# Emptying each tile of the feed-forward's up projection one tile later on VectorE

## Chip, core and metric

The kernel runs on one core of a Trainium2 chip. The metric is the device time of one execution in microseconds (us). Before the change, three runs gave a median of 3300.18 us (3292.87 to 3311.64).

## What is computed

The reference is a stack of transformer-like blocks on 512 tokens of width 1024. Two layers each end in a gated feed-forward of width 2752 with a short causal convolution (three taps over tokens), and this is the part that the change touches:

```
def conv_glu_ffn(xn, w_up, conv_w, conv_b, w_down):
    u, gt = split_cols(xn @ w_up, (D_FF, D_FF))
    u = causal_dwconv(u, conv_w, conv_b)
    return (jax.nn.silu(u) * gt) @ w_down
```

Before it, xn is a root-mean-square norm of the residual. The two layers have the same shapes. What follows them (a retention and attention block with a mixture of experts) is not touched.

## The kernel before

All is kept with features on the 128 partitions and 512 tokens along the free axis. A float32 product is made of three passes of the rounded format fp32r: the high part of the weights by the high part of x, high by low, and low by high. One **tile** of a projection is 128 output features by 512 tokens: 8 blocks of 128 input features by 3 passes, so 24 matmuls into one PSUM bank (`tile_products`, line 335 for the matmul). A weight chunk for one tile is 128x1024 values, 512 KB, loaded by SyncE into a ring of four (line 3361).

Each chunk is split on two engines before TensorE can use it. ScalarE casts it to its high part (`chunk_high`, line 302), and VectorE subtracts that from the chunk to get the low part, the **remainder** (`chunk_rest`, line 308). The split halves live in `chunk_split`, which has two places: the cast of chunk j therefore waits until tile j-2 has been multiplied. TensorE starts tile j when chunk j's remainder is done and one of four PSUM banks, used in turn, is free.

The up projection of a layer has 44 tiles, in groups of four: two tiles of u (the convolved half), then the two matching tiles of the gate. VectorE empties tile j in `up_out(j)` (lines 1467 to 1479). It first multiplies the bank by the norm's reciprocal roots into a scratch tile (line 1470). For a u tile it then makes the three taps of the convolution (lines 1473 to 1475), about 2.8 us in all; for a gate tile it multiplies by silu of the matching u tile into `hidden` (line 1478), about 1.4 us. The last instruction frees the bank (`bank_free`). ScalarE takes silu of a u tile in `silu_of(j)` (line 1407), once `up_out(j)` has freed its bank.

The order of the work is written out by hand, by engine. On VectorE (loop at lines 1502 to 1511), iteration j does the remainder of chunk j, then `up_out(j - 1)`, then at one iteration in four from j = 14 the low part of a finished hidden tile for the down projection (`x_rest`, line 322), and in 24 of the iterations one `ada_reduce` (lines 1018 to 1026: two instructions over a loaded 512 KB unit of another matrix). On ScalarE (loop at lines 1413 to 1426), iteration j casts chunk j, then takes silu of tile j-2, then at one iteration in four from j = 13 the high part of a hidden tile (line 314). At j = 2 ScalarE takes the square roots of the norm and VectorE turns them into reciprocals (line 396), so tiles 0 and 1 can be emptied only after that. Five times within the 44 tiles TensorE runs eight very narrow matmuls on the reduced unit (`ada_tile`, line 1035), and after tile 0 the norm's sum (line 379). GpSimd loads the units for `ada_reduce` (line 1006), each when an earlier unit has been used.

The down projection follows without a break (line 1376 is its matmul). Its first three output banks are others than the four of the up projection; before its fourth, TensorE waits for the last `up_out` (line 1366).

Of the kernel before, what the change touches and what calls it, by code (L numbers as in the profile page):

```python
# [155 lines left out]
def program(nc, d, out):  # L156

    ctx = ExitStack()
    with ctx:
# [55 lines left out]
        def vec(name, j=0, n=1):  # L215
            return vecs[:, VEC_AT[name] + j:VEC_AT[name] + j + n]
# [37 lines left out]
        def flat(ap):  # L254
            return ap.rearrange("p a b -> p (a b)")
# [41 lines left out]
        def chunk_high(act, lin, j):  # L297
            n = lin.c0 + j
            act.wait_ge(landed[n % RING], 16 * (n // RING + 1))
            act.wait_ge(chunk_used.sem, n + 1)  # L300
            at = (n % 2) * KB * P
            act.copy(chunk_split[:, 0, at:at + KB * P], flat(ring[:, n % RING])).then_inc(chunk_hi.sem, 1)  # L302

        def chunk_rest(dve, lin, j):
            n = lin.c0 + j
            dve.wait_ge(chunk_hi.sem, n + 1)
            at = (n % 2) * KB * P
            dve.tensor_tensor(chunk_split[:, 1, at:at + KB * P], flat(ring[:, n % RING]), chunk_split[:, 0, at:at + KB * P],  # L308
                              ALU.subtract).then_inc(chunk_taken.sem, 1)

        def x_high(act, lin, k, x, gain=None):
            dst = lin.split[0][k][:, 0:lin.tokens]
            if gain is None:
                act.copy(dst, x).then_inc(x_hi.sem, 1)
            else:
                act.activation(dst, x, ACT.Identity, scale=gain).then_inc(x_hi.sem, 1)
# [43 lines left out]
        def square(act, norm, k, x):  # L360
            act.activation(norm.squares[k][:, 0:norm.tokens], x, ACT.Square).then_inc(sq_ready.sem, 1)
# [24 lines left out]
        def take_roots(act, norm):  # L386
            act.wait_ge(sum_ready.sem, norm.b_sum + 1)
            ins = act.activation(norm.roots, banks[:, norm.bank, 0:norm.tokens], ACT.Sqrt, bias=eps[EPS], scale=1.0 / D)
            if norm.by_token is not None:
                ins = act.activation(norm.by_token, banks[:, norm.bank + 1, 0:norm.tokens // P], ACT.Sqrt, bias=eps[EPS],  # L390
                                     scale=1.0 / D)
            ins.then_inc(root_ready.sem, 1)
# [911 lines left out]
        def layer_end(layer, after=None):  # L1304
# [4 lines left out]
            n_up, n_down = 2 * FF_TILES, KB * DOWN_CHUNKS  # L1309
# [85 lines left out]
            def act(act):  # L1395
                if layer == 0:
                    act.activation(cond, vec("c", 0, 8), ACT.Silu).then_inc(cond_ready, 1)

                def prepare(j):
                    act.wait_ge(bank_free.sem, out.freed(j))  # L1400
                    x_high(act, up, j, x[j], gain[j])
                    square(act, norm, j, x[j])

                def silu_of(j):
                    if j % 4 < 2:
                        act.wait_ge(bank_free.sem, up.freed(j))
                        act.activation(silu[:, j % 4, :], conv[:, j % 4, :], ACT.Silu).then_inc(silu_ready.sem, 1)

                attention_act(act)
                for j in range(2, KB):  # L1410
                    chunk_high(act, out, j)
                    prepare(j - 2)
                for j in range(n_up):
                    chunk_high(act, up, j)
                    if j < 2:
                        prepare(KB - 2 + j)
                    elif j == 2:
                        take_roots(act, norm)
                    else:
                        if j == 3:  # L1420
                            silu_of(0)
                        silu_of(j - 2)
                    if j % 4 == 1 and 3 <= j // 4 < 11:
                        k = j // 4 - 3
                        act.wait_ge(bank_free.sem, up.freed(hidden_tile(k)))
                        x_high(act, down, k, hidden[:, k, :])
                for c in range(n_down):
                    g, m = c // KB, c % KB
                    chunk_high(act, down, c)
                    if g + 1 < DOWN_CHUNKS and m:  # L1430
                        for k in ks(g + 1):
                            if min(k % KB, KB - 2) == m - 1:
                                act.wait_ge(chunk_used.sem, down.used(KB * g - 1))
                                act.wait_ge(bank_free.sem, up.freed(hidden_tile(k)))
                                x_high(act, down, k, hidden[:, k, :])
                    if after and g == DOWN_CHUNKS - 1 and m >= 2:
                        next_x(act, m - 2)
                    if first and g == DOWN_CHUNKS - 1 and m >= 2:
                        first.square(act, m - 2)
                if first:  # L1440
                    first.act(act)
                if after:
                    beside = mixer.act(act, next_lin.freed)
                    for j in range(next_lin.n):
                        chunk_high(act, next_lin, j)
                        if j < 2:
                            next_x(act, KB - 2 + j)
                        elif j == 2:
                            take_roots(act, next_norm)
                        if j == 3 or j >= act_from:  # L1450
                            next(beside, None)
                    for _ in beside:
                        pass
# [6 lines left out]
            def dve(dve):  # L1460
# [6 lines left out]
                def up_out(j):  # L1467
                    i, n, bank, y = j // 4, j % 4, up.bank(j), turned[j % 2]
                    dve.wait_ge(chunk_used.sem, up.used(j))
                    L(dve.tensor_tensor(y, bank, norm.roots, ALU.mult))  # L1470
                    if n < 2:
                        c, w = conv[:, n, :], [vec(f"ffn_cw{layer}", 2 * i + n + FF_TILES * back) for back in range(3)]
                        L(dve.tensor_scalar(c, y, w[2], vec(f"ffn_cb{layer}", 2 * i + n), ALU.mult, ALU.add))
                        L(dve.scalar_tensor_tensor(c[:, 1:T], y[:, 0:T - 1], w[1], c[:, 1:T], ALU.mult, ALU.add))  # L1474
                        ins = dve.scalar_tensor_tensor(c[:, 2:T], y[:, 0:T - 2], w[0], c[:, 2:T], ALU.mult, ALU.add)
                    else:
                        dve.wait_ge(silu_ready.sem, base + 2 * i + n - 1)
                        ins = dve.tensor_tensor(hidden[:, 2 * i + n - 2, :], silu[:, n - 2, :], y, ALU.mult)
                    ins.then_inc(bank_free.sem, 1)
# [22 lines left out]
                for j in range(2, n_up):  # L1502
                    chunk_rest(dve, up, j)
                    if j == 2:
                        invert_roots(dve, norm)
                        up_out(0)
                    up_out(j - 1)
                    if j % 4 == 2 and 3 <= j // 4 < 11:
                        x_rest(dve, down, j // 4 - 3, hidden[:, j // 4 - 3, :])
                    for u in range(units_by(j - 1), units_by(j)):  # L1510
                        ada_reduce(dve, first_unit + u)
                dve.sem_inc(down_started, 1)
                chunk_rest(dve, down, 0)
                up_out(n_up - 1)
                for c in range(1, n_down):
                    g, m = c // KB, c % KB
                    chunk_rest(dve, down, c)
                    if g + 1 < DOWN_CHUNKS and m:
                        for k in ks(g + 1):
                            if min(k % KB, KB - 2) == m - 1:  # L1520
                                x_rest(dve, down, k, hidden[:, k, :])
                    if c == 3:
                        modulation(dve, layer)
                        if first:
                            first.constants(dve)
                    if g == DOWN_CHUNKS - 1 and m:
                        add_down(m - 1)
                        if after and m >= 2:
                            x_rest(dve, next_lin, m - 2, x[m - 2], next_gain[m - 2])
                            add_square(dve, next_norm, m - 2)  # L1530
                        if first and m >= 2:
                            first.add(dve, m - 2)
# [2017 lines left out]
```

## Time and profile before

| | |
|---|---|
| median of three runs | 3300.18 us (3292.87 to 3311.64) |
| span of the profiled execution, first to last instruction | 3300.1 us |
| first up projection (first matmul of it to first matmul of the down projection) | 618.48 to 873.18 us |
| second up projection | 1404.28 to 1658.88 us |
| TensorE busy over the span | 3120.8 us (95%) |
| VectorE busy over the span | 2292.4 us (69%) |

The profile gives the profiled execution's own time only as its span, 3300.1 us; that is 0.1 us under the median run, so sums against the one hold for the other. Engines are PE (TensorE), PEld (its weight load), DVE (VectorE), ACT (ScalarE), POOL (GpSimd) and SP (SyncE). In a timeline, a bracket at the end of a row gives how long the engine sat idle before it and which instruction released it; rows that follow each other on one line are merged with their count.

### The profile page before, as it was taken

Reading aid. Unit: us, or ns where it says so; the run is one execution under the profiler, and the core shown is the slowest. Engines: PE = TensorE matmul, PEld = TensorE weight load, DVE = VectorE, ACT = ScalarE, POOL = GpSimd, SP = SyncE. Lnnn points to the kernel's source line nnn. Section 1 sums busy time; section 2 is a strip of 40 time slices with the busy share of each in tenths; the row PEclk is TensorE's granted clock in tenths of the full one; section 3 lists DMA queues with packets and bytes.
Section 4 is the critical chain, followed back from the end, with each engine's and each line's share of the span. In section 5 each row is a group of like instructions: output and inputs, shape, how many; then the busy total and the mean of one; then the engine's idle time right before and its main releaser. Section 6 shows DMA issues by size and latency. Waiting matters only on the chain.

```text
span 3300.1 us, 44885 instructions
## 1 busy us (share of the span) xinstructions
PE 3120.8 (95%) x17105; PEld 2537.3 (77%) x17105; DVE 2292.4 (69%) x2269; ACT 1566.1 (47%) x1574; POOL 183.8 (6%) x214
## 2 busy tenths in 40 slices
PE   8979699999999789999999988889999999999998
PEld 7859587787887578778887766677888888888886
DVE  4664455677545654577735456679999999999997
ACT  3343233322234342422223224467777777777775
POOL 0000000000000000000000000101111111111110
PEclk9989899999999889999999997899999999999999
DMA  4210032344322112334323210679999999999996
GB/s 158 84 44 4 27 115 90 118 149 141 125 102 90 39 64 96 121 122 148 133 96 121 89 39 28 242 281 398 383 393 382 384 392 383 384 392 383 384 392 227
DMA packets 119374, 638.92 MB, mean 194 GB/s; under 512 B 13480, under 2 KB 13480, under 8 KB 69456
## 3 DMA queue, kind: packets, MB, share of 16 engines
q1 hardware_dynamic: 99168, 561.05, 44.1%
q0 software_dynamic: 20080, 76.04, 7.6%
q8 instruction: 97, 1.59, 0.2%
q14 instruction: 29, 0.24, 0.0%
HBM read 612.92 MB, written 24.12 MB: 193 GB/s over the span
## 4 chain that ended last, share of the span: by engine, by line
PE 86%; DVE 10%; ACT 1%; DMA 1%; issue 1%; PEldq 0%; DVEq 0%; SPq 0%; PEld 0%; POOL 0%; ACTq 0%; POOLq 0%
PE banks L335 31%; PE banks L2985 21%; PE banks L3002 10%; PE banks L1376 7%; PE banks L348 3%; PE banks L1834 3%; DVE chunk_split L308 1%; PE banks L2970 1%; PE banks L776 1%; PE banks L799 1%; PE banks L2991 1%; PE banks L2234 1%; DVE scratch L1474 1%; DVE scratch L396 1%; DVE scratch L1470 0%
## 5 line engine op out<-in xcount | busy, mean ns | idle before, releaser
L335 PE MATMUL banks<-x_scratch,chunk_split 128*128 128x512 f32 x3648 | 851.3, 394 | 36.3 <-DVE x_scratch L322 22.7
L335 PEld LDWEIGHTS banks<-x_scratch,chunk_split 128*128 128x128 f32 x3648 | 687.3, 189 | 193.1 <-issue 48.6
L302 ACT CAST chunk_split<-weight_ring 128x1024 fp32r<-128x1024 f32 x292 | 306.3, 1049 | 952.2 <-PE banks L335 719.2
L2985 PE MATMUL banks<-pair_split,rows 128*128 128x512 f32 x3072 | 717.2, 394 | 5.2 <-DVE pair_split L2633 3.5
L2985 PEld LDWEIGHTS banks<-pair_split,rows 128*128 128x128 f32 x3072 | 578.7, 189 | 137.9 <-issue 7.5
L308 DVE TENSOR_TENSOR chunk_split<-weight_ring,chunk_split 128x1024 fp32r<-128x1024 f32 x292 | 357.1, 1223 | 216.2 <-ACT chunk_split L302 207.1
L3002 PE MATMUL banks<-pair_split,hidden_t 128*128 128x512 f32 x1536 | 360.3, 393 | 2.5 <-DVE pair_split L2633 2.1
L3002 PEld LDWEIGHTS banks<-pair_split,hidden_t 128*128 128x128 f32 x1536 | 284.3, 188 | 65.5 <-DVE pair_split L2633 3.8
L2633 DVE TENSOR_TENSOR pair_split<-weight_ring,pair_split 128x2048 fp32r<-128x2048 f32 x128 | 290.4, 2289 | 35.9 <-ACT pair_split L2628 35.9
L2633 DVE TENSOR_TENSOR pair_split<-scratch,pair_split 128x2048 fp32r<-128x2048 f32 x128 | 290.5, 2289 | 31.1 <-ACT pair_split L2628 30.8
L2633 DVE TENSOR_TENSOR pair_split<-mixed,pair_split 128x2048 fp32r<-128x2048 f32 x128 | 291.3, 2290 | 24.6 <-ACT pair_split L2628 24.6
L2628 ACT CAST pair_split<-scratch 128x2048 fp32r<-128x2048 f32 x128 | 244.2, 1907 | 59.1 <-PE banks L2985 57.5
L2628 ACT CAST pair_split<-weight_ring 128x2048 fp32r<-128x2048 f32 x128 | 241.4, 1911 | 61.5 <-PE banks L2985 51.5
L2628 ACT CAST pair_split<-mixed 128x2048 fp32r<-128x2048 f32 x128 | 245.1, 1916 | 49.1 <-PE banks L2985 48.6
L1470 DVE TENSOR_TENSOR scratch<-banks,scratch 128x512 f32<-128x512 f32 x88 | 60.7, 690 | 119.1 <-PE banks L335 119.0
L1376 PE MATMUL banks<-x_down_hi,chunk_split 128*128 128x512 f32 x448 | 141.5, 395 | 0.0
L3240 POOL DMA_INDIRECT token_sums<-normed,tables x31 | 84.3, 2720 | 335.1 <-ACT normed L3078 302.8
L1376 PEld LDWEIGHTS banks<-x_down_hi,chunk_split 128*128 128x128 f32 x448 | 84.2, 188 | 19.7
L335 PE MATMUL banks<-x_mix,chunk_split 128*128 128x512 f32 x384 | 92.1, 399 | 0.0
L335 PE MATMUL banks<-x_queries,chunk_split 128*128 128x512 f32 x384 | 91.7, 397 | 0.0
L335 PE MATMUL banks<-x_proj,chunk_split 128*128 128x512 f32 x384 | 90.4, 397 | 0.0
L1376 PE MATMUL banks<-x_down_lo,chunk_split 128*128 128x512 f32 x224 | 88.2, 394 | 0.0
(661 smaller groups left out, 3581.0 us busy)
## 6 DMA issues: line engine op xcount, KB each, us to landing
weight_ring<-in_weights SPq DMA_DIRECT2D x292, 512.0 KB, 3.2
mixed<-in_w SPq DMA_DIRECT2D x128, 1024.0 KB, 7.5
weight_ring<-in_w SPq DMA_DIRECT2D x128, 1024.0 KB, 8.1
scratch<-in_w SPq DMA_DIRECT2D x128, 1024.0 KB, 8.9
mixed<-in_w_ada POOLq DMA_DIRECT2D x48, 512.0 KB, 3.8
token_sums<-tables POOLq DMA_DIRECT2D x1, 2560.0 KB, 9.3
residual<-in_x POOLq DMA_DIRECT2D x4, 512.0 KB, 6.6
projected<-in_mem POOLq DMA_DIRECT2D x2, 1024.0 KB, 5.2
```

The costliest lines, as they stand in the source:

```text
L302: act.copy(chunk_split[:, 0, at:at + KB * P], flat(ring[:, n % RING])).then_inc(chunk_hi.sem, 1)
L308: dve.tensor_tensor(chunk_split[:, 1, at:at + KB * P], flat(ring[:, n % RING]), chunk_split[:, 0, at:at + KB * P], ALU.subtract).then_inc( ...
L335: mm = pe.matmul(lin.bank(j), chunk_split[:, a, at + k * P:at + (k + 1) * P], lin.split[b][k][:, 0:lin.tokens], start=(k, a, b) == (0, 0, ...
L348: mm = pe.matmul(banks[:, into[tt], :], lin.split[b][k][:, tt * P:(tt + 1) * P], chunk_split[:, a, at:at + T], start=(k, a, b) == (0, 0, 0 ...
L1376: mm = pe.matmul(banks[:, DOWN_BANKS[m], :], chunk_split[:, a, at + (k % KB) * P:at + (k % KB + 1) * P], down.split[b][k], start=(k, a, b) ...
L1470: L(dve.tensor_tensor(y, bank, norm.roots, ALU.mult))
L1834: ins = pe.matmul(out(tt, c), lhs(tt, c), rhs(tt, c), start=True, stop=True)
L2628: act.copy(pair_split[s][:, 0, :], raw[r]).then_inc(pair_hi, 1)
L2633: dve.tensor_tensor(pair_split[s][:, 1, :], raw[r], pair_split[s][:, 0, :], ALU.subtract).then_inc(pair_lo, 1)
L2985: mm = pe.matmul(banks[:, n, :], rows[:, a, k, :], pair_split[k % SLOTS][:, b, n * T:(n + 1) * T], start=False, stop=(k, a) == (KB - 1, 1))
L3002: mm = pe.matmul(banks[:, 4 + n, :], hid_t[:, a, k, :], pair_split[c][:, b, at:at + T], start=(k, a, b) == (0, 0, 0), stop=(k, a) == (KB - ...
L3240: pool.indirect_dma_start(sums, bass.IndirectOffsetOnAxis(row_out, 0), y_tok, None, compute_op=ALU.add)\
```

## The change

On VectorE, iteration j empties tile j-2 in place of tile j-1. The reciprocal at j = 2 is followed by `up_out(0)` alone. The last two tiles go behind the remainders of the down projection's chunks 0 and 1. On ScalarE, silu follows one tile later too, and that of tile 41 goes behind the down projection's first cast. No instruction is added or removed.

```diff
@@ ScalarE @@
                     elif j == 2:
                         take_roots(act, norm)
                     else:
-                        if j == 3:
-                            silu_of(0)
-                        silu_of(j - 2)
+                        silu_of(j - 3)
...
                     chunk_high(act, down, c)
+                    if c == 0:
+                        silu_of(n_up - 3)
@@ VectorE @@
                     chunk_rest(dve, up, j)
                     if j == 2:
                         invert_roots(dve, norm)
-                        up_out(0)
-                    up_out(j - 1)
+                    up_out(j - 2)
...
                 dve.sem_inc(down_started, 1)
                 chunk_rest(dve, down, 0)
-                up_out(n_up - 1)
+                up_out(n_up - 2)
                 for c in range(1, n_down):
                     g, m = c // KB, c % KB
                     chunk_rest(dve, down, c)
+                    if c == 1:
+                        up_out(n_up - 1)
```

## Rows read from the trace of the kernel before

**Rows 1.** The page: busy time by engine, and the chain that ended last, by engine.
```profile
PE 3120.8 (95%) x17105; PEld 2537.3 (77%) x17105; DVE 2292.4 (69%) x2269; ACT 1566.1 (47%) x1574; POOL 183.8 (6%) x214
...
PE 86%; DVE 10%; ACT 1%; DMA 1%; issue 1%; PEldq 0%; DVEq 0%; SPq 0%; PEld 0%; POOL 0%; ACTq 0%; POOLq 0%
```

**Rows 2.** Windows, the two up projections: us, busy by engine, PEclk, DMA share, GB/s.
```profile
618.48:873.18 254.70, 247.87 (x1100) 202.22 (x1098) 185.14 (x237) 68.59 (x79) 11.61 (x22) 1.00 0.40 132
1404.28:1658.88 254.60, 247.77 (x1100) 202.23 (x1099) 185.14 (x237) 68.60 (x79) 10.57 (x20) 1.00 0.39 132
```

**Rows 3.** Waits in the first up projection: us in total, times, longest us.
```profile
POOL mixed L1006 <- DVEq L1028: 246.9, 20, 73.0
ACT chunk_split L302 <- PE banks L335: 150.7, 44, 5.7
DVE scratch L1470 <- PE banks L335: 59.3, 30, 3.8
...
PE banks L335 <- DVE chunk_split L308: 6.7, 9, 1.6
```

**Rows 4.** Groups of TensorE instructions in the second up projection: busy, mean ns | idle before.
```profile
L335 PE MATMUL banks<-x_scratch,chunk_split 128*128 128x512 f32 x1056 | 244.3, 391 | 6.8 <-DVE chunk_split L308 6.7
```

**Rows 5.** Timeline in the first up projection, start of the part with the reciprocal.
```profile
624.22 1.05 ACT L302 CAST chunk_split<-weight_ring 128x1024 fp32r<-128x1024 f32 x1 [3.29 <-PE banks L335]
...
625.37 1.23 DVE L308 TENSOR_TENSOR chunk_split<-weight_ring,chunk_split 128x1024 fp32r<-128x1024 f32 x1 [1.48 <-ACT chunk_split L302]
...
627.30 3.35 DVE L396 RECIPROCAL scratch<-scratch 128x512 f32<-128x512 f32 x1 [0.70 <-ACT scratch L388]
...
630.65 1.05 ACT L302 CAST chunk_split<-weight_ring 128x1024 fp32r<-128x1024 f32 x1 [3.38 <-PE banks L335]
...
636.21 1.22 DVE L308 TENSOR_TENSOR chunk_split<-weight_ring,chunk_split 128x1024 fp32r<-128x1024 f32 x1
...
637.58 12.73 PE L335 MATMUL banks<-x_scratch,chunk_split 128*128 128x512 f32 x55 [1.58 <-DVE chunk_split L308]
...
643.37 1.05 ACT L302 CAST chunk_split<-weight_ring 128x1024 fp32r<-128x1024 f32 x1 [5.48 <-PE banks L335]
```

**Rows 6.** Timeline, same stage, around a tile with the most VectorE work.
```profile
745.56 0.69 DVE L1470 TENSOR_TENSOR scratch<-banks,scratch 128x512 f32<-128x512 f32 x1 [1.46 <-PE banks L335]
745.62 1.05 ACT L302 CAST chunk_split<-weight_ring 128x1024 fp32r<-128x1024 f32 x1 [1.98 <-PE banks L335]
...
748.33 0.68 DVE L322 TENSOR_TENSOR x_down_lo<-projected,x_down_hi 128x512 fp32r<-128x512 f32 x1
748.45 0.63 ACT L1407 ACTIVATE scratch<-scratch 128x512 f32<-128x512 f32 x1 [1.78 <-DVE scratch L1475]
748.93 0.74 DVE L1020 SCALAR_TENSOR_TENSOR scratch<-mixed,tables,scratch 128x512 f32<-128x512 f32 x1
749.71 0.75 DVE L1022 SCALAR_TENSOR_TENSOR scratch<-mixed,tables,scratch 128x512 f32<-128x512 f32 x1
750.61 1.23 DVE L308 TENSOR_TENSOR chunk_split<-weight_ring,chunk_split 128x1024 fp32r<-128x1024 f32 x1
...
751.06 1.05 ACT L302 CAST chunk_split<-weight_ring 128x1024 fp32r<-128x1024 f32 x1 [1.98 <-PE banks L335]
...
751.98 8.22 PE L335 MATMUL banks<-x_scratch,chunk_split 128*128 128x512 f32 x35 [1.02 <-DVE chunk_split L308]
752.47 0.69 DVE L1478 TENSOR_TENSOR projected<-scratch 128x512 f32<-128x512 f32 x1
...
757.80 1.05 ACT L302 CAST chunk_split<-weight_ring 128x1024 fp32r<-128x1024 f32 x1 [5.69 <-PE banks L335]
```

**Rows 7.** Timeline of ScalarE, same stage: two casts with a narrow-matmul tile between them.
```profile
728.34 1.05 ACT L302 CAST chunk_split<-weight_ring 128x1024 fp32r<-128x1024 f32 x1 [2.52 <-PE banks L335]
734.74 1.05 ACT L302 CAST chunk_split<-weight_ring 128x1024 fp32r<-128x1024 f32 x1 [5.34 <-PE banks L335]
```

**Rows 8.** Waits of the SyncE queue in the first up projection: us, times, longest us.
```profile
SPq L3361 <- DVE chunk_split L308: 227.6, 44, 10.3
```

## The prediction

> **What bounds the kernel now.** I read the page first: TensorE is busy for 95% of the span, and 86% of the chain that ended last is TensorE's [rows 1]. So the change can be worth no more than TensorE's pauses in the stretches that it touches, unless it makes new ones. Those stretches are the two up projections. I took their windows from the first matmul of the up projection to the first of the down projection: 254.70 and 254.60 us, at a granted clock of 1.00, with VectorE busy for 185.14 us of each, 73% [rows 2]. Neither engine is full.
>
> The waits of the first stretch say what stops TensorE there: nine waits, 6.7 us in all, all on VectorE's remainder (line 308). The other way round, line 1470, the first instruction that empties a tile, waited 59.3 us for TensorE in 30 of its 44 times [rows 3]. So VectorE first waits for a tile to end, then empties it, and only then does the remainder that TensorE will need next. The second stretch has the same 6.7 us [rows 4].
>
> The timeline of a heavy tile shows the order [rows 6]. The tile ends at about 745.56. ScalarE casts the next chunk from 745.62 to 746.67, so its remainder could follow then. VectorE instead empties the tile until 748.33, makes the low part of a hidden tile until 748.93 and two instructions for the other matrix until 750.6, and does the remainder from 750.61 to 751.84. TensorE finished its tile in the meantime (the cast at 751.06 shows it) and starts the next at 751.98 only.
>
> **What these waits cost.** The casts mark the ends of tiles, since each waits for one. Undisturbed they are 5.44 us apart (745.62 to 751.06); after the late remainder the distance is 6.74 us (751.06 to 757.80), so a recorded idle time of 1.02 us cost 1.30 [rows 6]. The difference is overlap between matmuls of neighbouring tiles that is lost too. I therefore take the loss from the stretch, not from the idle times:
> - 44 tiles x 5.44 = 239.36 us
> - five tiles with the narrow matmuls behind them: 6.40 us between casts (728.34 to 734.74 [rows 7]), 0.96 more than 5.44, so 4.80 us
> - the norm's sum behind tile 0: 630.65 - 624.22 = 6.43 [rows 5], so 0.99 us
> - left of 254.70: 9.55 us; of 254.60: 9.45 us.
>
> Together **19.0 us** are due to late remainders, against 13.4 us of recorded idle (2 x 6.7). Of each 9.5, 1.84 us lie at the start, where two tiles took 643.37 - 630.65 = 12.72 us: there the reciprocal (3.35 us) and the emptying of tiles 0 and 1 all stand ahead of the remainder of chunk 3, which starts at 636.21 [rows 5].
>
> **The change, part by part.** No instruction is added or removed; the order changes.
>
> *VectorE, the steady loop.* After the remainder of chunk j, VectorE now empties tile j-2, which ended before that remainder could start. It no longer waits for tile j-1, and the next remainder has only that work ahead of it. Count from a cast's start at the end of tile j-2. The remainder is ready 2.38 us later (cast at 624.22, remainder to 626.60 [rows 5]). The heaviest work behind it is 5.05 us (745.56 to 750.61 [rows 6]), so VectorE is free at 7.43, and the next remainder, whose cast was ready at 5.44 + 1.05, ends at 8.66. TensorE wants it after two tiles, at 10.88: 2.2 us to spare, where it was late before. The other u tile of the group follows, without the low part (0.60 us from 748.33 to 748.93), but perhaps again with a unit: 8.66 + 4.45 + 1.23 = 14.34, against 16.32, so 2.0 us to spare. Then come two gate tiles of some 1.4 us (lines 1470 and 1478, 0.69 us each [rows 6]), which catch up. I find no late remainder in the loop: all of its share, 2 x 7.7 us, comes back.
>
> *VectorE, the start.* The reciprocal ends at 630.65, tile 0 takes 2.77 us (745.56 to 748.33 [rows 6]), and the remainder of chunk 3 ends at about 634.7. Tile 2 ends at about 630.6 + 5.44 = 636.0. So 1.3 us to spare where it was 1.4 late [rows 5]: the 1.84 us come back in both layers.
>
> *ScalarE's silu.* It goes behind the cast one tile later. It takes 0.63 us (748.45 [rows 6]) on an engine that is busy for 68.6 of 254.7 us [rows 2]. The gate tile that wants it is itself emptied a tile later, and by then the silu is done one whole cast earlier. The u tile is emptied 6.0 us after its end at worst (next part), and ScalarE comes to its silu 5.44 + 1.05 = 6.5 us after that end. Cost nothing; without that cover it would hold a cast, and with it a remainder that has 2.0 us to spare.
>
> *Banks.* A tile's bank comes free at 2.38 + 2.77 = 5.15 us after the tile's end, not at 2.77; for the second u tile at worst at 11.43 - 5.44 = 6.0. The tile that reuses it starts three tiles after that end, at 16.3 us. Ten us to spare. Cost nothing.
>
> *Queues.* The weight loads on SyncE wait for the remainders: 227.6 of 254.7 us of that queue's time [rows 8], so a transfer is never what is late, and the remainders come earlier, not later. The unit loads on GpSimd wait likewise for their slots (246.9 us [rows 3]) and move up by at most a tile, at a DMA share of 0.40 [rows 2]. The loads that GpSimd does for the next stage wait behind the loop, which now ends a tile's emptying earlier. Cost nothing.
>
> *The end of the stretch.* Chunk 1 of the down projection has its remainder ahead of the emptying of tile 43, so that is done 2.38 + 1.4 = 3.8 us after the tile's end. TensorE asks for it before its fourth down tile, 16 us after. Cost nothing.
>
> **Sum.** 3300.1 - 19.0 = 3281.1 us, 0.58% less, against the profiled span; the median run stands 0.1 us higher, so the same. The price of a late remainder has two readings in the rows: 13.4 us (recorded idle alone) and 19.0 (the stretch). I take 19.0, because the distance between casts is what the whole stage adds up from. A gain above 19.0 is excluded: then a tile would have to be shorter than 5.44, and the matmuls are not changed. What follows the stretches is released by TensorE's own progress, so it moves forward whole.
>
> **The rivals.**
> 1. *Only the recorded idle comes back.* The 0.3 us per wait above the idle time could be a cost of TensorE's that stays, for example if a remainder that comes just in time still lets the weight load start late. Speaks for it: the idle is what the profile records. Against: where the remainder is early, the casts stand 5.44 us apart with nothing added [rows 6]. 3300.1 - 13.4 = 3286.7.
> 2. *The gain is lost again.* Another wait takes the place, either VectorE's on ScalarE's cast or one in a later stage that hangs on something other than TensorE. Then 3300. Against: the 2 us to spare above; a wait of VectorE's on the cast is there already at the start of the stretch, 1.48 us, and held up nothing [rows 5].
> 3. *Banks run short, and it gets slower.* Emptying a tile later keeps its bank 2.38 us longer. If the 18 recorded waits were in truth waits for banks, each would grow by that: 18 x 2.38 = 42.8, so 3342.9 us. This decides from the point at which a bank comes free later than 16.3 us after its tile's end; the rows give 6.0 at worst, and name the remainder, not an emptied bank, for all of the idle time [rows 3, 4].
>
> The Trainium skill's Perfetto Trace Analysis has such a rule in its section "Optimization Strategy": a gap that repeats on the engine that should be saturated can mean that there is too little SBUF or PSUM for the next tile. By it this change, which holds PSUM longer, would go the way of rival 3; the trace does not agree, since its repeated gap ends with a remainder.
>
> **How the numbers follow.** Runs of this kernel lie 7.3 below to 11.5 us above their median, and 0.5% (16.5 us) is about what a measurement of it can tell from no change; that bound lies at 3283.7, only 2.6 us above the forecast. Chances: forecast 0.78, rival 1 0.12, rival 2 0.07, rival 3 0.03. With a median that can fall some 7 us to either side, about six in ten of the forecast's cases and a third of rival 1's end beyond 0.5%: 0.78 x 0.64 + 0.12 x 0.33 = 0.54 faster. Slower 0.04 (rival 3, and a little of rival 2). Same: 0.42. The range takes the forecast's and rival 1's scatter: 3272 to 3294.
>
> **What the changed profile should show.** In both stretches line 335's idle time on line 308 falls from 6.7 us to under 0.5, and the stretches shorten to about 245.2 us each. The casts stand 5.44 us apart but for the five narrow-matmul tiles and tile 1. Line 1470 no longer waits for TensorE; line 308 waits for the cast instead, in most tiles. VectorE's busy time stays at 185.1 us. Stretches of 248 us would mean rival 1; idle of TensorE behind lines 1475 or 1478 would mean rival 3; short stretches with an unchanged span would mean rival 2.

## The result and the profile after

The changed kernel takes 3283.51 us (median of 19 runs, 3270.04 to 3297.02) against 3299.24 us before (19 runs, 3288.13 to 3313.13). The ratio is 0.995 with a 95% interval of 0.9935 to 0.9964: 15.7 us less, 12 to 21 by the interval. The forecast was 3281.1.

First the two up projections, in windows of the changed kernel's trace (us, busy time by engine, granted clock, DMA share, GB/s), as in [rows 2]:

```profile
610.69:855.84 245.15, 245.15 (x1100) 203.01 (x1098) 183.63 (x237) 66.66 (x79) 11.62 (x22) 1.00 0.42 138
1385.36:1630.51 245.15, 245.15 (x1100) 202.99 (x1098) 183.65 (x237) 66.65 (x79) 10.55 (x20) 1.00 0.41 137
```

They last 245.15 us each, 9.55 and 9.45 less than before, together 19.0. TensorE is busy for the whole of both. The TensorE groups of the second stretch answer to [rows 4]:

```profile
L335 PE MATMUL banks<-x_scratch,chunk_split 128*128 128x512 f32 x1056 | 241.7, 390 | 0.0
```

Its idle time has gone from 6.8 us to 0.0. Where the waiting went is in the waits of the first stretch (us in total, times, longest us), which answer to [rows 3]:

```profile
POOL mixed L1006 <- DVEq L1028: 234.7, 20, 66.6
ACT chunk_split L302 <- PE banks L335: 177.1, 44, 5.3
DVE chunk_split L308 <- ACT chunk_split L302: 54.3, 30, 2.9
...
ACT scratch L1407 <- DVE scratch L1475: 0.8, 2, 0.5
```

Line 1470, the start of an emptying, no longer waits for TensorE at all (59.3 us before). VectorE now waits at the remainder, 30 times, for ScalarE's cast, which is the earliest that a remainder can start. Its free time has moved from a place ahead of the emptying, where it made the remainder late, to a place ahead of the remainder, where it is slack.

The timeline of a heavy pair of u tiles in the changed kernel, to be read beside [rows 6]:

```profile
728.11 1.05 ACT L302 CAST chunk_split<-weight_ring 128x1024 fp32r<-128x1024 f32 x1 [3.87 <-PE banks L335]
729.19 1.23 DVE L308 TENSOR_TENSOR chunk_split<-weight_ring,chunk_split 128x1024 fp32r<-128x1024 f32 x1 [2.89 <-ACT chunk_split L302]
730.34 0.68 DVE L1470 TENSOR_TENSOR scratch<-banks,scratch 128x512 f32<-128x512 f32 x1
...
733.09 0.68 DVE L322 TENSOR_TENSOR x_down_lo<-projected,x_down_hi 128x512 fp32r<-128x512 f32 x1
733.55 1.05 ACT L302 CAST chunk_split<-weight_ring 128x1024 fp32r<-128x1024 f32 x1 [4.39 <-PE banks L335]
...
735.37 1.23 DVE L308 TENSOR_TENSOR chunk_split<-weight_ring,chunk_split 128x1024 fp32r<-128x1024 f32 x1
...
738.99 1.05 ACT L302 CAST chunk_split<-weight_ring 128x1024 fp32r<-128x1024 f32 x1 [3.86 <-PE banks L335]
...
740.95 1.22 DVE L308 TENSOR_TENSOR chunk_split<-weight_ring,chunk_split 128x1024 fp32r<-128x1024 f32 x1
...
744.43 1.05 ACT L302 CAST chunk_split<-weight_ring 128x1024 fp32r<-128x1024 f32 x1 [3.86 <-PE banks L335]
```

The casts, which mark the ends of tiles, stand 5.44 us apart throughout. Even behind the heaviest work a remainder ends at 736.60 and 742.17, 2.4 and 2.3 us before the cast that marks the next tile's end.

**The profiled span shrank by more than the change gives.** It went from 3300.1 to 3271.4 us, 28.7. The stretches hold 19.0 of it. The first stretch began at 610.69 us in place of 618.48, so 7.8 us lie ahead of all edited code; 1.6 lie between the stretches and 0.3 behind them. The part ahead differs from execution to execution of the same code: its end lies between 609.2 and 633.4 us in the nine profiled kernels of this document, which all do the same up to there. These 24 us are about as much as the 25 and 27 us over which the runs of the two kernels scatter; what those nine executions take between and behind their stretches differs by some 8 us. So the medians are compared with an interval, and the experiments are read by the length of the stretches.

### The profile page after: what moved, and what is told of

It is laid out like the page before. It is cut to its first block, busy times and chain, and to the rows that moved or that the text cites. A ratio compares the mean times of both kernels' runs of the same rounds, so it can differ in the third digit from the quotient of the medians.

```text
span 3271.4 us, 44885 instructions
## 1 busy us (share of the span) xinstructions
PE 3108.4 (95%) x17105; PEld 2531.1 (77%) x17105; DVE 2289.1 (70%) x2269; ACT 1562.3 (48%) x1574; POOL 182.9 (6%) x214
## 4 chain that ended last, share of the span: by engine, by line
PE 90%; DVE 6%; DMA 1%; ACT 1%; issue 1%; SPq 0%; PEldq 0%; DVEq 0%; PEld 0%; POOL 0%; ACTq 0%; POOLq 0%
PE banks L335 35%; PE banks L2986 21%; PE banks L3003 10%; PE banks L1376 7%; PE banks L348 3%; PE banks L1835 2%; PE banks L2971 1%; PE banks L776 1%; PE banks L799 1%; PE banks L2992 1%; PE banks L2235 1%; PE banks L2979 0%; DVE chunk_split L308 0%; DMA mixed<-in_w 0%; PE banks L2294 0%
## 5 line engine op out<-in xcount | busy, mean ns | idle before, releaser
L335 PE MATMUL banks<-x_scratch,chunk_split 128*128 128x512 f32 x3648 | 845.0, 393 | 22.8 <-DVE x_scratch L322 22.8
L1376 PE MATMUL banks<-x_scratch,chunk_split 128*128 128x512 f32 x384 | 87.4, 389 | 0.0
```

The lines of the kernel that those rows point to most:

```text
L335: mm = pe.matmul(lin.bank(j), chunk_split[:, a, at + k * P:at + (k + 1) * P], lin.split[b][k][:, 0:lin.tokens], start=(k, a, b) == (0, 0, ...
L1376: mm = pe.matmul(banks[:, DOWN_BANKS[m], :], chunk_split[:, a, at + (k % KB) * P:at + (k % KB + 1) * P], down.split[b][k], start=(k, a, b) ...
```

## Experiments

### One part at a time

**Only the start.** Tiles 1 and 2 go behind the remainder of chunk 3; from then on the order is that of before.

```diff
                     if j == 2:
                         invert_roots(dve, norm)
                         up_out(0)
-                    up_out(j - 1)
+                    else:
+                        if j == 3:
+                            up_out(1)
+                        up_out(j - 1)
```

> Only the start is changed: behind the reciprocal VectorE empties tile 0 alone, tiles 1 and 2 go behind the remainder of chunk 3, and from there on the order is that of the kernel before. If each late remainder costs on its own, the 1.84 us at the start come back and the other 7.7 us of each up projection stay: 252.8 us per stretch, from 254.7, with 8 waits of TensorE on the remainder (line 308) in place of 9, and about 3.7 us off the whole. If the start is all that mattered, the stretches are about 245.2 us. If only recorded idle time comes back, 253.1 us.

**Only the loop.** The changed kernel, with the start as before.

```diff
                     if j == 2:
                         invert_roots(dve, norm)
-                    up_out(j - 2)
+                        up_out(0)
+                        up_out(1)
+                    elif j > 3:
+                        up_out(j - 2)
```

> Only the loop is changed: tiles 0 and 1 are both emptied ahead of the remainder of chunk 3, as before, and each later tile one tile later. If each late remainder costs on its own, one wait of TensorE is left (1.6 us recorded, 1.84 us of time) and each stretch is about 247.0 us, 7.7 less than before. Together with the kernel in which only the start is changed the two savings should add up to the whole, 9.5 us. If a late start also sets the later waits up, the stretches come out nearer 245.2 or nearer 254.7 than that.

Windows of the two stretches, first the kernel with only the start changed:

```profile
611.08:863.88 252.80, 247.54 (x1099) 202.29 (x1098) 185.17 (x237) 68.59 (x79) 11.61 (x22) 1.00 0.40 133
1396.13:1648.91 252.78, 247.51 (x1099) 202.28 (x1098) 185.24 (x237) 68.58 (x79) 10.56 (x20) 1.00 0.39 132
```

then the one with only the loop changed:

```profile
619.65:866.63 246.98, 245.43 (x1100) 202.93 (x1098) 183.71 (x237) 66.57 (x79) 11.60 (x22) 1.00 0.41 137
1400.79:1647.77 246.98, 245.44 (x1100) 202.92 (x1098) 183.72 (x237) 66.57 (x79) 10.56 (x20) 1.00 0.41 136
```

and the one row of TensorE's waits on the remainder in the first stretch of the kernel with only the start changed:

```profile
PE banks L335 <- DVE chunk_split L308: 5.1, 8, 1.0
```

Start alone: 252.8 us, 1.9 saved. Loop alone: 247.0 us, 7.7 saved. Together 9.6 in the first stretch, against 9.55 for the whole change (9.4 and 9.45 in the second). The late remainders are independent of each other, and what they cost is the longer distance between tiles, not the recorded idle time: the loop alone saves 7.7 us, although it removes only eight recorded waits of 5.1 us in all (those of the row above; the second stretch lists nine, 5.3 us in all). The single runs took 3293.52 and 3289.34 us, each inside the scatter.

### Is it the emptying, or the work behind it?

The order of before is kept, tile j-1 in iteration j. Only VectorE's other work is moved ahead of the emptying, into the wait for the tile. Tiles 0 and 1 are still both emptied ahead of chunk 3's remainder, so the words of the expectation on tile 0 alone do not fit this edit; the 1.84 us that it leaves at the start do.

```diff
                         up_out(0)
-                    up_out(j - 1)
                     if j % 4 == 2 and 3 <= j // 4 < 11:
                         x_rest(dve, down, j // 4 - 3, hidden[:, j // 4 - 3, :])
                     for u in range(units_by(j - 1), units_by(j)):
                         ada_reduce(dve, first_unit + u)
+                    up_out(j - 1)
```

> The emptying stays where it was before (tile j-1 in iteration j, so behind the end of that tile); only the other work of VectorE's iteration, the low part of a hidden tile and the unit's reduction, is moved ahead of it, into the time in which VectorE waits for the tile; and tile 0 alone follows the reciprocal, so tile 1 stands behind the remainder of chunk 2 only. Theory: a remainder is late when more than 5.44 us of VectorE's work lie between a tile's end and it. Emptying a u tile and the remainder are 2.77 + 1.23 = 4.0 us, so nothing is late in the loop; at j = 2 both tiles 0 and 1 are still emptied ahead of the remainder of chunk 3 (1.84 us stay). Stretches of 247.0 us, the whole about 15 us under before. If it is the wait for tile j-1 by itself that costs, so that emptying a tile later is what is needed, the stretches stay near 254.7 or 252.8 us.

Windows of the two stretches:

```profile
617.01:863.96 246.95, 245.42 (x1099) 202.89 (x1098) 183.74 (x237) 68.57 (x79) 11.61 (x22) 1.00 0.42 138
1394.89:1641.92 247.03, 245.44 (x1099) 202.89 (x1098) 183.75 (x237) 68.59 (x79) 10.56 (x20) 1.00 0.41 136
```

and rows of the waits in the first:

```profile
DVE scratch L1470 <- PE banks L335: 53.3, 28, 3.4
...
PE banks L335 <- DVE chunk_split L308: 1.5, 1, 1.5
```

247.0 us, as much as the loop of the change gives, although VectorE still waits 53.3 us for tiles to end. The ratio to before is 0.9967 (0.9945 to 0.9989), 11 us less and 4 to 18 by the interval, which agrees with the 15.3 us of the two stretches. So the wait for tile j-1 is not the cost by itself. What costs is the amount of VectorE work that stands between a tile's end and the remainder: a u tile's emptying and the remainder are 4.0 us and fit into 5.44; with the extras they don't.

### How late may a bank be freed?

The changed kernel, with tile j-4 emptied in iteration j in place of j-2.

```diff
-                        silu_of(j - 3)
+                        if j >= 5:
+                            silu_of(j - 5)
...
-                    if c == 0:
-                        silu_of(n_up - 3)
+                    if c <= 2:
+                        silu_of(n_up - 5 + c)
...
-                    up_out(j - 2)
+                    if j >= 4:
+                        up_out(j - 4)
...
-                up_out(n_up - 2)
+                up_out(n_up - 4)
...
-                    if c == 1:
-                        up_out(n_up - 1)
+                    if 1 <= c <= 3:
+                        up_out(n_up - 4 + c)
```

> Tile j-4 is emptied in iteration j, two tiles later than in the changed kernel, and silu follows. A bank is then freed by the emptying that stands behind the remainder of the chunk for the very tile that reuses the bank. Theory: banks have time to spare. The bank of a u tile comes free 2.4 + 2.8 = 5.1 to 5.2 us after the end of the tile two before its user, and is wanted at 5.44; where a unit's reduction has gone before, VectorE is 1 us later and the bank up to 1 us late. So the stretches are 245.2 us or a little more, up to 249 us, and any idle time of TensorE is ended by lines 1475 or 1478, none by 308. If banks were what TensorE waited for, holding each two tiles (10.9 us) longer would cost several us per group of four tiles, and the stretches would be above 270 us.

Windows of the two stretches:

```profile
633.41:879.49 246.08, 246.08 (x1099) 202.06 (x1098) 179.84 (x231) 65.39 (x77) 11.61 (x22) 1.00 0.42 141
1407.35:1653.39 246.04, 246.04 (x1100) 202.01 (x1099) 179.86 (x231) 65.38 (x77) 10.55 (x20) 1.00 0.42 138
```

and one row of the waits in the first (line 1476 is line 1475 of the kernel before, the end of a u tile's emptying):

```profile
PEld banks L335 <- DVE scratch L1476: 2.1, 10, 0.3
```

246.1 us: 0.9 more than the changed kernel, with no idle time of TensorE recorded; some tiles end 0.1 us late. Ten weight loads (PEld) waited up to 0.3 us for an emptying, so here the banks have nothing left to spare. Holding each bank 10.9 us longer than the change does is next to free. The single run took 3296.23 us, but its first stretch began at 633.41 us, 22.7 us later than in the changed kernel's profile, in code that no kernel here alters.

### Adding VectorE work to each order

In each u tile's emptying the first instruction of the convolution is done four times in place of once, with the same outcome: 3 x 0.58 = 1.74 us more per u tile, 38 us per stretch.

```diff
-                        L(dve.tensor_scalar(c, y, w[2], vec(f"ffn_cb{layer}", 2 * i + n), ALU.mult, ALU.add))
+                        for _ in range(4):
+                            L(dve.tensor_scalar(c, y, w[2], vec(f"ffn_cb{layer}", 2 * i + n), ALU.mult, ALU.add))
```

In the kernel before:

> The kernel before, with the first instruction of the convolution (0.55 us) done four times in place of once for each u tile: 1.74 us more of VectorE's work per u tile, 22 of them in each stretch, 38 us. Theory: in the order of before, all VectorE work between a tile's end and the next remainder beyond 5.44 us stalls TensorE, so 2.77 + 1.74 + 1.23 = 5.7 us makes nearly every u tile late, and those with extras by 1 to 3 us. Added up tile by tile from the durations of the profile, each stretch is about 281 us, 26 more than before, with some 20 waits; the whole about 52 us longer. If VectorE had free time to take it up (it is busy 73% of the stretch), the stretches stay near 254.7 us.

In the changed kernel:

> The same three additional instructions per u tile in the changed kernel. Theory: its remainders have about 2 us to spare, and VectorE can catch up in the gate tiles, so only the worst pairs of u tiles are late: added up from the durations, about 0.8 us at the start and 1.5 us where two u tiles in a row both carry extras, 247.5 us per stretch, 2.3 more than the changed kernel without them; the same 38 us of work that costs the order of before 26 us. The whole stays about 14 us under before. If the changed order had won only because the work happened to fit, and has no slack of its own, each stretch is 10 us or more above 245.2.

In the kernel that empties tile j-4:

> The same three additional instructions in the kernel that empties tile j-4 in iteration j. The bank of a u tile now comes free 2.4 + 2.77 + 1.74 = 6.9 us after the end of the tile two before its user, where it is wanted at 5.44: so here banks must be what TensorE waits for. Added up from the durations: about 270 us per stretch, 16 waits of up to 1.8 us, ended by lines 1475 and 1478. With the changed kernel's 247.5 us for the same work this gives the price of emptying too late, the mechanism of the rival by which the change would have been slower. If banks do not bind even here, the stretch is near 247 us.

Windows of the stretches, the kernel before with the added work:

```profile
617.28:907.13 289.85, 261.38 (x1099) 210.51 (x1098) 220.43 (x303) 68.51 (x79) 11.60 (x22) 0.95 0.35 116
1436.08:1729.08 293.00, 263.36 (x1099) 211.92 (x1098) 220.41 (x303) 68.53 (x79) 10.55 (x20) 0.95 0.34 116
```

the changed kernel with it:

```profile
609.19:858.95 249.76, 246.20 (x1099) 202.42 (x1098) 217.88 (x302) 69.99 (x81) 11.60 (x22) 1.00 0.40 134
1387.59:1637.30 249.71, 246.14 (x1100) 202.42 (x1098) 217.86 (x302) 70.00 (x81) 10.55 (x20) 1.00 0.40 134
```

and the one that empties tile j-4:

```profile
610.16:881.21 271.05, 250.41 (x1100) 201.83 (x1099) 212.04 (x292) 66.65 (x77) 11.62 (x22) 1.00 0.39 128
1411.70:1682.72 271.02, 250.31 (x1099) 201.82 (x1098) 212.05 (x292) 66.54 (x77) 10.56 (x20) 1.00 0.38 126
```

with this row of the waits in its first stretch (line 1477 is line 1475 of the kernel before, the end of a u tile's emptying):

```profile
PE banks L335 <- DVE scratch L1477: 20.6, 16, 1.6
```

The same 38 us of VectorE work cost 35 to 38 us per stretch in the order of before, 4.6 us in the changed order and 25 us where the bank is freed at the last moment. VectorE is busy for about 87% of the changed kernel's stretch then (217.9 of 249.8), so it is not the amount of work that decides but what stands behind it. Whole runs: before with the work 1.0185 of before (1.0155 to 1.0214), so 51 to 71 us longer; in the profiled executions the two stretches add up to 73.6 us and the span grew by 68.9 (3369.0 against 3300.1); the changed kernel with it 0.9953 (0.9925 to 0.9981), still faster than the kernel before without it.

Two of the three sums were too small. For the changed kernel 247.5 was expected and 249.7 to 249.8 measured. The casts show three late remainders of 0.85, 1.73 and 1.76 us; the sum had the first two (0.8 and 1.5) and left out the third, the first chunk of the down projection behind the heavy pair of tiles 40 and 41, which counts into the stretch (tiles late by 0.1 to 0.2 us make up the rest of the 4.6). This last one shows as its own wait:

```profile
PE banks L1376 <- DVE chunk_split L308: 1.5, 1, 1.5
```

For the kernel before the sum, 281, fell short by 9 and 12 us, and there the granted clock is 0.95 in place of 1.00 [rows 2]. The third kernel came out as expected, 271 with 16 waits, and names the bank.

The clock is the part that the sum did not have. Rows of TensorE's timeline in the first stretch of the kernel before with the added work, four pauses and the matmuls after them:

```profile
639.86 18.87 PE L335 MATMUL banks<-x_scratch,chunk_split 128*128 128x512 f32 x72 [5.09 <-DVE chunk_split L308]
...
737.53 5.69 PE L335 MATMUL banks<-x_scratch,chunk_split 128*128 128x512 f32 x24 [2.16 <-DVE chunk_split L308]
745.20 16.60 PE L335 MATMUL banks<-x_scratch,chunk_split 128*128 128x512 f32 x72 [1.19 <-DVE chunk_split L308]
...
821.56 7.31 PE L335 MATMUL banks<-x_scratch,chunk_split 128*128 128x512 f32 x24 [2.23 <-DVE chunk_split L308]
```

and windows of 4 us behind three of those pauses (the granted clock is the third number from the end):

```profile
737.00:741.00 4.00, 3.47 (x15) 2.92 (x16) 3.82 (x7) 0.00 (x0) 0.00 (x0) 1.00 0.71 239
...
821.50:825.50 4.00, 3.94 (x11) 3.14 (x12) 2.34 (x3) 0.00 (x0) 0.00 (x0) 0.59 0.91 288
...
639.80:643.80 4.00, 3.94 (x9) 3.15 (x10) 2.35 (x3) 0.39 (x1) 0.00 (x0) 0.50 0.54 153
```

Behind the pause of 5.09 us the clock is 0.50, the lower of the two levels (1.2 GHz); behind one of 2.23 us it is 0.59, a mean over both levels, and the tile takes 7.31 us in place of 5.69, so 1.6 more. Behind a pause of 2.16 us it is 1.00 in one place. In the first stretch six distances between casts are 9.2 to 9.6 us, where an equally late remainder with the clock at 1.00 gives 7.85: 6 x 1.6 = 9.6 us. Behind the pause of 5.09 us 72 matmuls took 18.87 us, where they take 16.60 at a clock of 1.00: 2.3 more. Together the lower clock cost about 11.9 us, and the sum was short of 8.9: the clock accounts for the whole shortfall, and the rest of the sum was some 3 us too large; why stays open.

## Why the prediction came out

**The loss in the rows of before: right.** It was worked out as 19.0 us from the stretches, in preference to the 13.4 us of recorded idle. The stretches shrank by 19.0 us, to 245.15 where 245.2 was said. The first rival (only the recorded idle comes back, stretches of 248) falls: the stretches are 3 us shorter than that.

**The slack of the new order: right.** 2.2 and 2.0 us to spare were worked out for the two heavy u tiles, and the trace has 2.4 and 2.3. With 1.74 us per u tile added, the order was late in three places only, so the slack is about of that size and not more.

**The start: right.** 1.84 us per layer were said to lie there, and the kernel with only the start changed got 1.9 and 1.8 back.

**Silu, banks and queues at nothing: right.** ScalarE's silu waited 0.8 us in all in the first stretch, and TensorE was busy for all 245.15 us of both, so neither a bank nor a queue held it: 44 tiles of 5.44 us with 4.80 for the narrow matmuls and 0.99 for the norm's sum are 245.15, and nothing is left over. That banks are not what decides is shown by the kernel that empties tile j-4 (0.9 us lost). That they can be is shown by the same kernel with the added work: 26 us per stretch lost against the changed kernel without it, every wait ended by an emptying. The third rival's mechanism exists; the change is 10 us away from it. The rule on repeated gaps in the Trainium skill's Perfetto Trace Analysis, section "Optimization Strategy", says that such gaps can mean too little SBUF or PSUM; here the 18 gaps were a producer that stood behind an emptying in one engine's order, and holding PSUM longer removed them.

**The second rival, gain lost later: not seen.** What lies between and behind the stretches took 1.6 and 0.3 us less, no more. The measured whole, 15.7 us with an interval of 12 to 21, holds the 19.0.

**Small things that were off.** VectorE's busy time in a stretch was said to stay at 185.1 us and is 183.6. The same 237 instructions lie in the stretch before and after. Line 1470 takes 683 ns in place of 690, 0.3 us in all; the rest is that records of neighbouring instructions overlap more in the new order (added up one by one, they take about 190.6 us before and 190.3 after). That is bookkeeping of busy time and bears on nothing in the forecast. And 0.58% was expected where the median says 0.48%; with single runs scattered over 25 us the two cannot be told apart, and the bound of 0.5% lies between them.

Not settled: why the code ahead of the first stretch takes from 609 to 633 us in different executions. In the window of 180 to 420 us the granted clock was 0.85 to 0.86 in the four executions that came to the first stretch at 609 to 611 us, 0.82 to 0.84 in the four that came at 617 to 620, and 0.73 in the one that came at 633.41. So the two go together; whether the clock is the cause there or follows other waits was not tried.

## What to carry to other kernels

Where one engine both prepares the next tile's operand and empties the last tile, put the operand first and the emptying behind it, one tile later if a bank can be spared: work that waits for a tile's end should not stand ahead of work on which the next tile waits. Size such a loss by the distance between the events that mark the ends of tiles, not by recorded idle time, which here was 30% too small. Before giving up the order, see whether other work of the same engine can be moved into its wait: that alone brought 7.7 of 9.5 us.

## What the runs showed of the hardware

- A pause of TensorE can cost more than its length. In the kernel with the most delay (the one before, with the work added), six of the eight pauses of 1.9 to 2.2 us in the first stretch were followed by a granted clock of 0.58 to 0.67 over the next 4 us and a tile longer by about 1.6 us, two (2.16 and 2.21 us) were not; a pause of 5.09 us was followed by 0.50. The 32 pauses of up to 1.6 us in the two stretches of the kernel that empties tile j-4, with the work added, left it at 1.00 over both.
- The length of the pause alone does not decide that. The second stretch of the kernel with the most delay again has six of eight pauses of 1.9 to 2.2 us that were followed by a lower clock (0.57 to 0.68). One of the two that were not is the first row here; the pause of 1.19 us that came next was followed by 0.59, and its 72 matmuls took 18.22 us, where those behind the pause of 1.19 us in the first stretch took 16.60:

```profile
1687.65 5.69 PE L335 MATMUL banks<-x_scratch,chunk_split 128*128 128x512 f32 x24 [2.16 <-DVE chunk_split L308]
1695.30 18.22 PE L335 MATMUL banks<-x_scratch,chunk_split 128*128 128x512 f32 x72 [1.19 <-DVE chunk_split L308]
...
1695.30:1699.30 4.00, 4.00 (x11) 3.13 (x12) 2.29 (x3) 0.00 (x0) 0.00 (x0) 0.59 0.53 156
```

- A recorded idle time of 1.02 us cost 1.30 us [rows 6], and one tile in the kernel before was late by 0.4 us (casts 5.86 us apart) with 0.14 us of idle that the list of waits does not name (TensorE busy for 0.56 of the 0.70 us from 653.90). Both are 0.28 us more than the idle. That fits the records of matmuls, which last 390 ns each while 24 of them take 5.44 us, so that neighbours overlap by some 0.16 us (an estimate from these two numbers); the other 0.1 us was not traced.
